# Expert weights in 2 MB chunks, and tokens of four experts gathered straight into the turned layout

## The reference, cut to what matters

```python
logits = xt @ w_router + b_router            # 32 experts, each token picks 4
top_v, top_i = lax.top_k(logits, TOP_K)
gates = jax.nn.softmax(top_v, axis=-1)
...
gu = xb @ w_gate_up[e] + b_gate_up[e]        # w_gate_up[e]: 1024 x 2048 float32
gate, up = gu[:, :D_EXPERT], gu[:, D_EXPERT:]
gate = jnp.minimum(gate, SWIGLU_LIMIT)
up = jnp.clip(up, -SWIGLU_LIMIT, SWIGLU_LIMIT)
act = (up + 1.0) * (gate * jax.nn.sigmoid(SWIGLU_ALPHA * gate))
return act @ w_down[e] + b_down[e]           # w_down[e]: 1024 x 1024 float32
```

## Time and profile before

| what | value |
|---|---|
| median of three executions | 1468.39 us (1465.54 to 1471.56) |
| the profiled execution, its own time | 1469.54 us |
| its span, first to last instruction | 1467.8 us |
| mean granted clock of TensorE | 0.983 |
| TensorE busy | 1403.6 us, 96% of the span |
| VectorE, ScalarE, GpSimd busy | 444.7, 247.4, 70.2 us |
| moved by the DMA engines | 488.16 MB |
| packets of SP's queue | 137864 |

### The profile page before, as it was taken

How to read it: one execution, slowest core, us unless ns; L and a number is a source line. 1 busy time by engine, 2 the same in 40 slices (tenths; PEclk the granted TensorE clock), 3 DMA queues, 4 the chain that set the end, 5 groups by cost and what they waited for, 6 DMA issues and landing times.

```text
span 1467.8 us, 17038 instructions
## 1 busy us (share of the span) xinstructions
PE 1403.6 (96%) x6448; PEld 719.8 (49%) x6448; DVE 444.7 (30%) x1104; ACT 247.4 (17%) x455; POOL 70.2 (5%) x55
## 2 busy tenths in 40 slices
PE   9999998996999899999999999999999999999996
PEld 8888876785887533333333333333333333333332
DVE  2765256897412511211211211112112011121113
ACT  2113453312100201101101011011010111110103
POOL 1000001473000000000000000000000000000000
PEclk9999999998999599999999999999999999999999
DMA  9444347796576299999999999999999999999995
GB/s 247 131 143 148 114 135 236 236 374 214 172 244 251 106 364 367 417 414 422 415 419 418 414 423 415 418 418 415 423 415 417 420 415 421 417 416 420 415 419 216
DMA packets 148484, 488.16 MB, mean 333 GB/s; under 512 B 12531, under 2 KB 78283, under 8 KB 113575
## 3 DMA queue, kind: packets, MB, share of 16 engines
q1 hardware_dynamic: 137864, 459.95, 79.9%
q0 software_dynamic: 4224, 23.37, 4.6%
q10 hardware_dynamic: 6354, 4.29, 1.2%
HBM read 476.64 MB, written 11.19 MB: 332 GB/s over the span
## 4 chain that ended last, share of the span: by engine, by line
PE 74%; DVE 7%; DMA 6%; SPq 6%; ACT 4%; issue 1%; ACTq 1%; POOL 0%; POOLq 0%; DVEq 0%
PE bank L276 72%; SPq L332 6%; DMA xnT<-in_w_gate_up 4%; DVE ring L1405 3%; PE bank L785 3%; DMA xnT<-in_w_down 1%; DVE ring L1402 1%; DMA ring<-ac_dram 1%; DVE conv L1402 1%; ACT plain L687 1%; ACT plain L702 0%; DMA out<-ring 0%; DVE ring L1382 0%; DVE ring L1368 0%; ACT plain L551 0%
## 5 line engine op out<-in xcount | busy, mean ns | idle before, releaser
L276 PE MATMUL bank<-ring,plain 128*64 128x512 f32 x2304 | 520.4, 597 | 12.4 <-ACT plain L702 10.1
L276 PEld LDWEIGHTS bank<-ring,plain 128*64 128x64 f32 x2304 | 156.5, 136 | 323.3 <-issue 307.5
L276 PE MATMUL bank<-xnT,ring 128*128 128x264 f32 (+1 forms) x1168 | 264.1, 387 | 3.5 <-ACT plain L523 3.4
L276 PEld LDWEIGHTS bank<-xnT,ring 128*128 128x128 f32 (+1 forms) x1168 | 219.2, 189 | 45.0 <-issue 6.9
L1515 DVE TENSOR_TENSOR xT<-xT,bank 128x264 f32<-128x264 f32 x128 | 54.9, 429 | 488.6 <-PE bank L276 487.6
L276 PE MATMUL bank<-conv,plain 128*64 128x512 f32 (+3 forms) x416 | 169.9, 610 | 5.4 <-DVE plain L1487 3.6
L276 PEld LDWEIGHTS bank<-conv,plain 128*64 128x64 f32 (+2 forms) x416 | 54.7, 167 | 95.8 <-issue 90.0
L276 PE MATMUL bank<-ring 128*128 128x264 f32 (+3 forms) x520 | 80.2, 335 | 9.5 <-DVE ring L1382 8.4
L1520 DVE TENSOR_SCALAR plain<-bank 128x512 f32<-128x512 f32 x32 | 22.0, 688 | 218.1 <-PE bank L276 218.1
L697 ACT ACTIVATE plain<-plain 128x512 f32<-128x512 f32 x32 | 20.1, 629 | 363.0 <-DVE plain L1520 363.0
L276 PEld LDWEIGHTS bank<-ring 128*128 128x128 f32 (+1 forms) x520 | 68.0, 170 | 22.8 <-issue 14.2
(11 more groups left out here) (266 smaller groups left out, 869.5 us busy)
## 6 DMA issues: line engine op xcount, KB each, us to landing
ring<-in_w_gate_up SPq DMA_DIRECT2D x192, 1024.0 KB, 19.3
ring<-in_w_down SPq DMA_DIRECT2D x96, 1024.0 KB, 20.6
ring<-in_w_in SPq DMA_DIRECT2D x36, 1024.0 KB, 5.2
ex<-in_w_gate_up SPq DMA_DIRECT2D x16, 1024.0 KB, 21.8
plain<-in_w_gate_up SPq DMA_DIRECT2D x16, 1024.0 KB, 23.0
conv<-in_w_gate_up SPq DMA_DIRECT2D x16, 1024.0 KB, 24.3
xnT<-in_w_gate_up SPq DMA_DIRECT2D x16, 1024.0 KB, 25.6
ring<-in_w_proj_b SPq DMA_DIRECT2D x8, 1024.0 KB, 7.5
```

Source lines behind the costliest of these rows:

```text
L276: return nc.tensor.matmul(out, w, x, start=start, stop=stop)
```

## The change

The chunks of weights become 2 MB, 12 to a pair, in 8 slots. A chunk of gate/up weights takes two consecutive rows of the matrix to a partition, a chunk of down weights four, so both are 16 KB in one piece in HBM and in a partition. The row order that this gives is followed by the columns of the tokens and of the hidden values that are used as stationary operand, which are read with a step of 2 and of 4 elements. Two of the 8 slots lie across other tiles and are filled ahead in halves, by `load_half`. A chunk is counted as used after the matmuls of both its k (or all four).

The tokens of four experts are gathered at a time, with the operands exchanged: the tokens are the stationary operand (128 columns) and `pick` (256 columns) the moving one, so that the result has the turned layout at once, and the 8 transposes and half of the copies go. A pair does half of it, four of the eight groups of 128 columns, for the next four experts. The first gather, ahead of the loop, does all eight. DVE makes `pick` for four experts in every other pair, and `pg` by a comparison of its own. `n_final` is loaded by SP at the end.

```diff
-MSLOT = 16
+WIDE = 2 * SLOT
+MSLOT = 8
+QUADS = E // 4
+QUAD = 4 * SLOTS
-CHUNKS = 24
+CHUNKS = 12
...
             def load_chunk(j, c, slot):
-                if c < 2 * KT:
-                    k = c % KT
-                    src = w_gu[2 * j + c // KT, P * k:P * k + P, :]
-                    dst = stream[slot]
+                if c < KT:
+                    k = c % 4
+                    src = w_gu[2 * j + c // 4, 2 * P * k:2 * P * k + 2 * P, :].rearrange("(p s) n -> p (s n)", s=2)
                 else:
-                    k = (c - 2 * KT) // 2
-                    src = w_dn[2 * j + c % 2, 2 * P * k:2 * P * k + 2 * P, :].rearrange("(k p) n -> p k n", p=P)
-                    dst = stream[slot].rearrange("p (k n) -> p k n", k=2)
-                sp.dma_start(dst, src).then_inc(w_landed[slot], 16)
+                    k = (c - KT) // 2
+                    src = w_dn[2 * j + c % 2, 4 * P * k:4 * P * k + 4 * P, :].rearrange("(p s) n -> p (s n)", s=4)
+                sp.dma_start(wide[slot], src).then_inc(w_landed[slot], 16)
+
+            def load_half(c, s):
+                src = w_gu[c // 4, 2 * P * (c % 4):2 * P * (c % 4) + 2 * P, :].rearrange("(p s) n -> p s n", s=2)[:, s, :]
+                sp.dma_start(wide[c][:, SLOT * s:SLOT * s + SLOT], src).then_inc(w_landed[c], 16)
...
-                        for chunk in (4, 5, 6, 7, 11):
+                        for chunk in (2, 3):
                             load_chunk(0, chunk, chunk)
...
+            sp.wait_ge(S["x_filled"], 6 * n_passes)
+            sp.dma_start(n_final, a["norm_final"].rearrange("(o d) -> o d", o=1).to_broadcast([P, D])).then_inc(S["final_loaded"], 16)
...
-            def gather(buf, h, tiles):
-                for t in tiles:
-                    n = ROWS[t]
-                    ins = mm(p_xg[h][:, :], buf[0:n, t].rearrange("p w s -> p (w s)"),
-                             u_tok[0:n, t, 512 * h:512 * h + 512], t == 0, t == 2)
+            u_cols = u_tok.rearrange("p t (k i s) -> p t k s i", i=P, s=2)
+
+            def gather(out, c):
+                for t, n in enumerate(ROWS):
+                    ins = mm(out[:, QUAD * (c % 2):QUAD * (c % 2) + QUAD], u_cols[0:n, t, c // 2, c % 2, :],
+                             pick[0:n, t].rearrange("p w s -> p (w s)"), t == 0, t == 2)
+                if c % 2:
+                    ins.then_inc(S["xt_filled"], 1)
...
             def first_gather(g):
                 pe.wait_ge(S["pick_ready"], g + 1)
-                for h in range(2):
-                    gather(pick[0], h, (0, 1, 2))
-                for h in range(2):
-                    turn_tokens(g, h)
+                for c in range(KT):
+                    gather(p_xt[c // 2], c)
...
             def turn_hidden(m):
+                cols = ha.rearrange("p (i s) -> p s i", s=4)
                 for c in range(4):
-                    ins = turn(p_ht[:, P * c:P * c + P], ha[:, P * c:P * c + P], P)
+                    ins = turn(p_ht[:, P * c:P * c + P], cols[:, c, :], P)
...
-                gather(pick[1 - r], 0, (0, 1, 2))
-                gather(pick[1 - r], 1, (0, 1))
-                pe.wait_ge(S["ht_ready"], 2 * i + 1)
-                turn_hidden(2 * i + 1)
-                gather(pick[1 - r], 1, (2,))
-                pe.wait_ge(S["gu_emptied"], 2 * i + 2)
-                turn_tokens(g + 1, 0)
-                pe.wait_ge(S["ht_ready"], 2 * i + 2)
-                down(0)
-                turn_tokens(g + 1, 1)
-                for kk in range(1, 4):
-                    down(kk)
+                pe.wait_ge(S["gu_emptied"], 2 * i + 1)
+                if not final:
+                    pe.wait_ge(S["pick_ready"], g + 2)
+                    for c in range(3):
+                        gather(p_xt[c // 2], 4 * r + c)
+                    pe.wait_ge(S["ht_ready"], 2 * i + 1)
+                    turn_hidden(2 * i + 1)
+                    gather(p_xt[1], 4 * r + 3)
...
+                pe.wait_ge(S["ht_ready"], 2 * i + 2)
+                down(0)
+                if final and r:
+                    pe.wait_ge(S["x_taken"], 6 * p + 2)
+                    turn_rest(p, 2)
+                    pe.wait_ge(S["x_taken"], 6 * p + 6)
+                    down(1, True)
+                else:
                     down(1)
```

More of the change, by code:

```diff
@@ L158, in build @@
         y_out = plain_t[:, 3584:4608]
[L159 to L163, removed]
+        pick = plain_t[:, 6656:6656 + 3 * QUAD].rearrange("p (t w s) -> p t w s", t=3, w=4)
+        n_final = ring[:, 3 * WIDE:3 * WIDE + D]
+        u_tok = conv_t[:, SLOT:SLOT + 3 * D].rearrange("p (t d) -> p t d", t=3)
         rows_out = u_tok
@@ L752, in _ @@
                     nc.scalar.copy(pgt[0:E, :], p_pg[0:E, 0:NT]).then_inc(S["pgt_ready"], 1)
-                with act.Fori(0, PAIRS - 1) as q:
-                    take_pair(p, q, False)
-                take_pair(p, PAIRS - 1, True)
+                with act.Fori(0, QUADS // 2 - 1) as q:
+                    for u in range(2):
+                        for r in range(ROUND):
+                            take_pair(p, 2 * q + u, u, r)
+                for u in range(2):
+                    for r in range(ROUND):
+                        take_pair(p, QUADS - 2 + u, u, r, u == 1)
             def square_rows(t):
@@ L1081, in arrived @@
                     pe.wait_ge(w_landed[slot], landed_by)
-                    return stream[slot]
+                    return wide[slot]
                 def bias(x):
@@ L1110, in pair @@
-                pe.wait_ge(S["xt_ready"], 2 * g + 2)
-                pe.wait_ge(S["pick_e_ready"], g + 1)
+                    w = [arrived(KT + 2 * kk + x) for x in range(2)]
+                    for h, c in [(h, c) for h in range(2) for c in range(4)] if halves else \
+                            [(h, c) for c in range(4) for h in range(2)]:
+                        for x in range(2):
+                            ins = mm(p_y[h][SLOTS * x:SLOTS * x + SLOTS, :],
+                                     ht[:, x, c, SLOTS * kk:SLOTS * kk + SLOTS],
+                                     w[x][:, D * c + 512 * h:D * c + 512 * h + 512], kk == c == 0, kk == 1 and c == 3)
+                            if c == 3 and h:
+                                ins.then_inc(S["w_used"], 1)
+                        if halves and c == 3 and not h:
+                            ins.then_inc(S["y_half"], 1)
@@ L1169, in _ @@
                     ins.then_inc(S["pg_filled"], 1)
-                with pe.Fori(0, PAIRS // ROUND - 1) as q:
+                with pe.Fori(0, QUADS // 2 - 1) as q:
+                    for u in range(2):
+                        for r in range(ROUND):
+                            pair(p, 2 * q + u, u, r)
+                for u in range(2):
                     for r in range(ROUND):
-                        pair(p, q, r)
-                pair(p, PAIRS // ROUND - 1, 0)
-                pair(p, PAIRS // ROUND - 1, 1, True)
+                        pair(p, QUADS - 2 + u, u, r, u == 1)
             items = PAIRS * n_passes
@@ L1542, in work @@
                     swiglu(i, 1)
-                    pick_experts(0 if final else j + 1)
-                with dve.Fori(0, PAIRS // ROUND - 1) as q:
+                    pick_experts(0 if final and r else j + 1)
+                with dve.Fori(0, QUADS - 1) as q:
                     for r in range(ROUND):
                         work(q, r)
-                work(PAIRS // ROUND - 1, 0)
-                work(PAIRS // ROUND - 1, 1, True)
+                work(QUADS - 1, 0, True)
+                work(QUADS - 1, 1, True)
             def add_rows(t, h):
```

178 lines of the change are left out of this document (82 added, 96 removed).

## The result

| what | before | after |
|---|---|---|
| median, this comparison (4 executions each) | 1467.18 us (1465.54 to 1471.56) | 1476.83 us (1475.65 to 1479.35) |
| ratio after/before, 95% interval | | 1.0063 [1.0037, 1.0090] |
| the profiled execution, its span | 1467.8 us | 1475.6 us |
| mean granted clock of TensorE | 0.983 | 0.971 |

The forecast was 1462.5 us with a range of 1451 to 1476. The change makes the kernel slower by 0.4 to 0.9%, and the median lies 0.8 us over the range.

The account below looks back on a forecast made before the run. The DMA engines were taken to set the end. Packets -20.3, later first release +8.8, dry stretch +2.0 and tail +3.6 sum to -5.9 us, giving 1462.5 us as forecast median, range 1451 to 1476.

Parts of the forecast that it names:

- (b): First gather, ahead of the loop: low clock until 514 for 4.5 of 8 groups, then fast; loop starts at 520.6, not 512.86.
- The first release comes later: Ahead of the loop: wider `pick`, longer first gather and coarser slot release delay the first waiting load, +8.8 us (+6.5 to +15).
- a gather that runs at the low clock to its end: First gather: one of three signs named in advance that would show the forecast wrong.
- The packets: Weight stream: 16 KB packets stay whole, 4.91 us per 2 MB chunk, 184 chunks in 903.4 us, -20.3 us.
- The dry stretch: Early in the loop: DMA engines run out of released slots once, 6.4 us against about 4.5 before, +2.0 us (0 to +4).
- The tail: After the last landing: `down(1)` is 32 instructions, 7.2 us, and waits for both its chunks, +3.6 us.
- The load of `n_final`: At the end: issued about 1.5 us before the last landing, took 8.8 us; hidden, else its lateness adds in full.
- What TensorE saves in a pair: Loop: 56.9 us a pair against 58.9 of the DMA engines; 1.3 us gained, hidden behind them.
- A: Rival, weight stream: packets gain nothing over 8 KB or are cut to 8 KB; 12.9 us more, 1475.4; chance 0.15.
- B: Rival, weight stream: long packets go slower, for instance 5.12 us a chunk, +38.6, 1501; chance 0.06.
- C: Rival, loop: strided stationary reads cost their full bound, 59.5 us a pair, TensorE sets the end; +12, 1474; chance 0.05.
- D: Rival, better case: 4.85 us a chunk, or clock up after 10 us of gather, or both; 1450 to 1457; chance 0.22.

Follow-up runs that it names:

- e4: Kernel before with only the 2 MB chunks, their row order and the late `n_final` load, keeping the old gather: 1463.48 us, ratio 0.9948.
- e3: Kernel after, its first gather multiplying by dense columns of `xT` in place of the 0/1 matrix `pick`: 1471.92 us, one execution.
- e6: Kernel before with only the new four-expert gather and its buffers, keeping the old 1 MB chunks: 1488.55 us, ratio 1.0124.
- e7: Kernel after with `turn_rest` of the last 8 rows moved ahead of `down(0)` in the last pair: 1473.83 us, one execution.
- e5: Kernel after, first gather's same 48 instructions reordered: 128-row tiles of four groups, then their 8-row tiles, then the other four groups: 1464.55 us, ratio 0.9969.
- e1: Kernel after plus 19 extra TensorE products, results thrown away, in waits ahead of the loop: 1460.96 us, ratio 0.9935.
- e2: Kernel before plus 19 extra TensorE products, results thrown away, in waits ahead of the loop: 1464.73 us, ratio 0.9954.
- e10: Kernel before with 2 MB chunks alone, 19 extra TensorE products ahead of the loop, and the last rows turned earlier: 1455.94 us, ratio 0.9923.

## Why the prediction was wrong, step by step

**The step that failed** is (b) of "The first release comes later". It took from the earlier trace rows the time at which the clock rose, 514, and carried it over to another instruction stream, in which 4.5 of 8 groups would be slow and the rest fast. The time of the rise can't be carried over: with the old gather it was 514 in before and about 506 in e4, and in the changed gather, in the order of the changed kernel, it did not come at all in four traces of four (after, e3, e6, e7). The step's own upper bound, "+15 if it never does before the loop", is what happened: first gather to first waiting load +15.6 where +8.3 was taken (e5: with the order of the tiles changed 20.5 us from the start to the load, +2.8 over before; e1: 19.2). The price of a group was right, 3.16 us measured at the low clock (25.30/8) against 3.26. The prediction gave the two ends a range and no reason for the middle. It named "a gather that runs at the low clock to its end" as a sign of being wrong, but the case belonged among the rivals with a chance of its own. With +15 in place of +8.8 the sum is +0.3 and not -5.9. From there to the measured +7.8 it is +1.0 in this step (0.4 and 15.6 against 15), +2.6 of an earlier part that ended later, +2.4 in the stream and +1.5 in the tail.

The Trainium skill's page "TensorE: Matmul & The Clock Gate", Part 1, says that for modelling the penalty of the ramp is under 1% of a typical kernel's span. Here the low clock cost the first gather 11.6 us (25.30 against 13.67 in e1), 0.8% of 1475.6, which agrees; all that e1 gained is 15.9 us, 1.1%, a little over it. Either is larger than the whole effect that was to be forecast.

**The other terms.** The packets: 4.901 us a chunk against 4.91, 184 x 4.901 = 901.8, -21.9 where -20.3 was forecast; 16 KB packets stay whole, as this answer for 1310 to 1320 of after shows (292 - 32 = 260 packets with weights, 4.26 MB, 16 KB each):

```profile
DMA packets 292, 4.26 MB, mean 426 GB/s; under 512 B 32, under 2 KB 32, under 8 KB 32
```

The Trainium skill's page "DMA: Bandwidth & Descriptors", Measured, has 425 GB/s for one transfer of 16 MB. The 426 to 429 of these slices are close to it.

The dry stretch: idle shares of 0.57 and 0.33 in two windows of 5 us make 4.5 us against 3.4 by the earlier trace rows for before, so +1.1 of the +2.0; it came once, as said, at 575 to 585. But the time that is neither packet pace nor forecast grew by 6.0 us in all (917.3 - 901.8 = 15.5 against 9.5). The larger part is at the end: from 1444 the DMA share is 0.54, then 0.46, 0.48 and 0.12 in windows of 2 us, though the last chunk lands only at 1452.35; that is 5.1 us of idle share, against 1.7 in the last windows of before (0.84 and 0.11). In the trace's records of the single packets 16 of them are under way at 1443.35 and eight from 1445.35 to 1449.35, each 0.61 us long as before: half of the 16 engines are done some us ahead of the others. About 1.5 us of the 6.0 stay unassigned.

The tail: +5.1 against +3.6, the clock and the order of `turn_rest` (e7). The load of `n_final` did no harm: SP issued it at 1453.28, 0.9 us behind the last landing where 1.5 ahead of it was forecast, and with the queue empty it landed after 3.6 us in place of 8.8. What TensorE saves in a pair: 57.28 us against 56.9, hidden as forecast. Start of the gather: +3.0, of which the wider `pick` is 0.4 (0.96 us against 0.56), the rest the difference from one execution to the next.

**The rivals.** A (no gain over 8 KB, or cut) and B (slower packets) fell by 4.901 us a chunk. C (strided reads cost) fell by 57.28 us a pair. D fell too: a chunk took 4.901 us and not 4.85, and the clock rose later than forecast and not sooner. The measured 1476.8 lies near the 1475.4 of A and the 1474 of C, which is chance: neither mechanism was there. The gain of the packets did arrive, -15.9 us from the first waiting load to the last landing, and the 15.6 us at the first gather gave it back.

Two sums of the working are off by a little and move nothing: the row of 4 KB packets gives 2.557 us for 1 MB and not 2.559, and the prediction's own terms put the last landing at 1440.1 and not 1440.6 (1449.63 - 20.3 + 8.8 + 2.0). The 0.107 us for a load in rival C stands beside no row.

What was right in the method is the frame: that the end is the DMA engines' end, so the first release counts one to one, and savings within a pair count nothing.

## What to carry to other kernels

When a stream of DMAs sets the end, all that delays its start counts in full: look at what runs once, ahead of the loop, with the DMA share at zero, before adding work there for the sake of the loop. Do not carry the time at which TensorE's clock rose over to another instruction stream; price both levels, and if the order of the same instructions is free, try another: here it helped to put those with 8 rows together behind those with 128. And a saving on an engine that waits anyway can be left out of the change altogether: here the chunks alone did as well as both parts.

## What the runs showed of the hardware that was not expected

- TensorE, busy without a gap for 25.3 us, kept the granted clock of 0.50 to the end of the gather, in after, e3, e6 and e7 alike (25.29 or 25.30 us each time). The same 48 instructions in another order took 13.14 us, with the clock at 0.50 in 502 to 505 and at 0.89 in 505 to 508 (e5). With the clock already up when it began, the interleaved order did not bring it down (e1: 13.67 us).
- The clock also went down while TensorE was busy without a gap with products of 32 columns: the windows show 0.50 in 484 to 487 of e2 and, with transposes behind them, 0.70 in 487 to 490 of e1.
- What the moving operand holds, nearly all zeros or dense numbers, made no difference to the 25.30 us (e3).
- The same twelve instructions of the old gather took 11.49 us in before and 7.43 in e4, as the clock rose at about 506 there: the time of the rise varies from one execution to the next, or from one kernel to the next, even behind the same wait of 3.58 us.
- DMAs of 2 MB in rows of 16 KB went at 4.901 us each, 428 GB/s. At the end of such a stream the 16 engines did not finish together: the mean share was near one half for the last 6 to 8 us, where with 1 MB chunks it fell from 1.02 to 0.11 within 4 us. The size of the chunks alone does not do it: in e10, with 2 MB chunks too but a last landing 21.5 us after its issue in place of 34.1, the share went from 1.04 (1417 to 1419) to 0.67 and 0.06 in the next two windows of 2 us.
